# Applying RMS norms behind the products they feed, and moving adaLN modulation chunks to VectorE

## The reference

```
m = silu(cond) @ w_mod[layer] + b_mod[layer]        # 6 x 1024: shift, scale, gate for each of two sub-layers
h = rms_norm(x, g) * (1 + scale) + shift
layer 0: x += gate * even_mixer(h);   x += gate * swiglu(h)             # FF: 1024 -> 2816 -> 1024
layer 1: x += gate * odd_mixer(h);    x += gate * top2_of_8_experts(h)  # a router reads h
y = rms_norm(x, g_f)
rms_norm(x, g) = x * rsqrt(mean(x * x) + eps) * g
```

## Time and profile before

| | |
|---|---|
| time, median of 3 runs | 2267.85 us (2267.14 to 2271.6) |
| time of the profiled execution | 2261.82 us |
| its span | 2260.2 us, mean granted clock of TensorE 0.926 |
| matmuls and transposes | 12138 records on PE |
| DMA | 288 MB, 128 GB/s over the span |

### The profile page before, as it was taken

One profiled execution on the slowest core, in us unless ns is written; L12 is line 12 of the kernel. 1 busy time (PEld: TensorE's weight loads), 2 busy tenths in 40 slices (PEclk: granted clock), 3 DMA queues, 4 the chain that ended last, 5 costly groups with the idle time before them and its releaser, 6 DMA issues.

```text
span 2260.2 us, 34401 instructions
## 1 busy us (share of the span) xinstructions
PE 1978.4 (88%) x12138; PEld 1691.3 (75%) x12139; DVE 1144.8 (51%) x1934; ACT 759.0 (34%) x1265; POOL 327.8 (15%) x344
## 2 busy tenths in 40 slices
PE   4699999999999999987878974997797988887985
PEld 2495586999999986953333943997786988887983
DVE  1436733223322323157886455346575877685435
ACT  1325322222122222222232341334443655553321
POOL 1301102000000002059600020001101001101021
PEclk9799999999999999997687997998998999998996
DMA  7323425335521244223000142357756889866433
GB/s 217 112 75 118 143 80 181 102 85 139 148 75 49 77 139 146 76 95 96 0 1 0 38 123 82 95 159 199 227 146 197 232 240 272 244 182 174 113 91 137
DMA packets 439474, 288.38 MB, mean 128 GB/s; under 512 B 20858, under 2 KB 428634, under 8 KB 439300
## 3 DMA queue, kind: packets, MB, share of 16 engines
q1 hardware_dynamic: 425124, 248.75, 37.9%
q0 software_dynamic: 12272, 34.50, 5.2%
q10 hardware_dynamic: 1904, 3.13, 0.5%
HBM read 262.86 MB, written 23.47 MB: 127 GB/s over the span
## 4 chain that ended last, share of the span: by engine, by line
PE 73%; DVE 13%; issue 8%; ACT 2%; POOL 2%; DMA 1%; ACTq 1%; DVEq 1%; POOLq 0%
PE ps L1076 15%; PE ps L1078 15%; PE ps L1077 15%; PE ps L1081 11%; PE ps L1082 4%; PE ps L1119 4%; DVE vp L1928 2%; PE ps L1169 2%; PE ps L1382 1%; DVE lo L1670 1%; PE ps L1399 1%; POOL tmp L2314 1%; DVE am L1989 1%; DVE hot L2129 1%; PE ps L1493 1%
## 5 line engine op out<-in xcount | busy, mean ns | idle before, releaser
L1076 PE MATMUL ps<-h_both,hi 128*128 128x320 f32 x1728 | 541.8, 314 | 43.2 <-issue 24.2
L1670 DVE TENSOR_TENSOR lo<-raw,hi 128x1024 fp32r<-128x1024 f32 (+3 forms) x442 | 452.4, 1051 | 179.0 <-ACT hi L674 175.3
L1077 PE MATMUL ps<-h_both,hi 128*128 128x320 f32 x1728 | 539.1, 312 | 0.0
L1078 PE MATMUL ps<-h_both,lo 128*128 128x320 f32 x1728 | 538.7, 312 | 0.0
L674 ACT ACTIVATE hi<-raw 128x1024 fp32r<-128x1024 f32 (+3 forms) x442 | 397.1, 919 | 386.7 <-PE ps L1078 233.2
L1076 PEld LDWEIGHTS ps<-h_both,hi 128*128 128x128 f32 x1728 | 328.8, 190 | 47.5 <-issue 34.1
L1081 PE MATMUL ps<-h_both,hi 128*128 128x256 f32 (+2 forms) x1056 | 294.7, 366 | 59.7 <-issue 50.0
L1077 PEld LDWEIGHTS ps<-h_both,hi 128*128 128x128 f32 x1728 | 329.2, 191 | 0.2 <-issue 0.2
L1078 PEld LDWEIGHTS ps<-h_both,lo 128*128 128x128 f32 x1728 | 329.0, 190 | 0.0
L1081 PEld LDWEIGHTS ps<-h_both,hi 128*128 128x128 f32 x1056 | 210.5, 199 | 69.8 <-issue 51.3
L1082 PE MATMUL ps<-h_both,lo 128*128 128x128 f32 (+2 forms) x1056 | 257.1, 243 | 0.0
(11 more groups left out here) (315 smaller groups left out, 2414.9 us busy)
## 6 DMA issues: line engine op xcount, KB each, us to landing
raw<-in_moe_w_dram SPq DMA_DIRECT2D x160, 512.0 KB, 5.4
raw<-in_w_mod_dram SPq DMA_DIRECT2D x96, 512.0 KB, 4.5
raw<-in_moe_w_dram SPq DMA_DIRECT2D x64, 384.0 KB, 3.6
raw<-in_ff_w_dram SPq DMA_DIRECT2D x40, 512.0 KB, 5.0
raw<-in_moe_w_dram SPq DMA_DIRECT2D x64, 320.0 KB, 3.7
y_rows<-zeros POOLq DMA_DIRECT2D x22, 512.0 KB, 4.5
raw<-in_moe_w_dram SPq DMA_DIRECT2D x32, 256.0 KB, 2.9
raw<-in_ev_w_in_dram SPq DMA_DIRECT2D x12, 512.0 KB, 4.5
```

The lines of the kernel that those rows point to most:

```text
L1076: pe.matmul(out, w_hi, v_hi, start=first, stop=False, skip_group_check=True)
L1077: pe.matmul(out, w_hi, v_lo, start=False, stop=False, skip_group_check=True)
L1078: return pe.matmul(out, w_lo, v_hi, start=False, stop=last, skip_group_check=True)
L1670: dve.tensor_tensor(lo[c % 2][:, parts[h]], raw[ring_of(c) % 4][:, parts[h]], hi[c % 2][:, parts[h]].bitcast(F32), ALU.subtract).then_inc( ...
```

## The change

Three things are done together.

1. **Norms 0, 1 and 2 are applied behind the product.** h is x·`amod` without `rs`: ACT writes the high part straight from `xT` (`scaled_hi`, two segments), DVE the low part (`scaled_lo`, two STT, scalar_tensor_tensor). POOL's step and x·rs are gone. The eviction multiplies PSUM by `rs` on DVE (`raw_out`; in FF in `ff13_evac`). `rs` is made while the first step runs; PE waits for `n_var` ahead of half 1, as the sums of norms 1 and 2 now lie in banks 2 and 3. Norm 3 keeps its place, but its affine part moves from POOL to DVE and ACT.
2. **The shift goes through the product as two more moving columns.** `h_wide` has eight columns ahead of the 640; the last two hold the shifts of the two kinds of token, so half 0 has 322 columns, and shift·W comes out beside the product. DVE copies it to `bias`; ACT adds it in place (Identity, Gelu, Sigmoid, or in FF the SiLU), and in FF a DVE STT adds the other one and takes the product.
3. **32 of the 48 chunks leave PE's row form.** Chunks 0 to 7 and 12 to 19 stay. Chunks 8 to 11 are done in EIN's steps 0 to 3, and 20 to 47 in FF's steps `FF_STEPS` (of 38: 1, 3, 5, 7 and 9 to 32), by 16 DVE instructions each (`mod_acc_of`): for both conditioning vectors, over eight k tiles, 256 columns times a scalar per partition, added up. Two steps on, ahead of half 1, PE adds over partitions with four fp32 matmuls (`mod_sum`: 128x128 weights, two columns of ones), and DVE adds b_mod (`mod_bias`). Their weights come through the ring between the product's chunks (`MOD_AT`).

With this PE's loops over FF are written out, squares and ones-matmuls of norm 2 go into FF's last down steps, and the runs of chunks ahead of FF, OIN, the heads and the router are gone. Of the diff, the core:

```diff
+FF_STEPS = [1, 3, 5, 7] + list(range(9, 33))
+BY_PE = list(range(8)) + list(range(12, 20))
+MOD_AT = [0] * 8 + [EIN + 2 + i for i in range(4)] + [EOUT + 2] * 8 + [ff_step(s) for s in FF_STEPS]
+        h_wide = place("h_wide", [P, 2, KT, HW], F32R)
...
+            def scaled_hi(layer, which, k):
+                for lo_t, hi_t, cond in SEGS:
+                    last = act.activation(hh[:, k, lo_t:hi_t], xT[:, k, lo_t:hi_t], ACT.Identity, scale=amod[:, layer, which, k, cond:cond + 1])
+                last.then_inc(n_hi, 1)
...
+            for k in range(4):
+                square(1, k, (evac, 2 * (EOUT + k // 2 + 1)))
+            act.wait_ge(gemm_out, 2 * (EOUT + 4))
+            shift_hi(1, 0, 1)
+            for k in range(KT):
+                if k < 6:
+                    scaled_hi(0, 1, k)
+                if k < 4:
+                    square(1, 4 + k, (evac, 2 * (EOUT + (4 + k) // 2 + 1)))
...
+                    act.wait_ge(f_raw, at + h + 1)
+                    for lo_t, hi_t, cond in HALF_SEGS[h]:
+                        part = sil(h)[:, lo_t - TH * h:hi_t - TH * h]
+                        last = act.activation(part, part, ACT.Silu, bias=bias[:, 0, 0, cond:cond + 1])
...
+            def mod_sum(q, bank):
+                pe.wait_ge(mod_acc, among(q) + 1)
+                for i in range(2):
+                    for c in range(2):
+                        at = 336 + 4 * i + 2 * c
+                        last = pe.matmul(ps[:, bank, at:at + 2], acc_of(q)[:, c, i * P:(i + 1) * P], ones[:, 0:2], start=True, stop=True, skip_group_check=True)
+                last.then_inc(mod_summed, 1)
...
                 for h in range(2):
+                    if h and ready:
+                        pe.wait_ge(n_var, 2)
+                    if h and q < JT and summed_in(s) is not None:
+                        mod_sum(summed_in(s), bank + 2)
...
+                for m in range(KT):
+                    ff2(m, n0 + N_UP + m, s0 + JT + m, 2 * JT * (f + 1), 2 * (n0 + JT - 1) if m < 2 else None)
+                    if f and m >= 2:
+                        norm_mm(2, m - 2)
+
+            norm_mm(2, KT - 2)
+            norm_mm(2, KT - 1)
...
-            mods(28, 2)
-            pe.wait_ge(evac, 2 * OIN)
-            norm_pe(2)
-            mods(30, 2, True)
...
+            def mod_acc_of(q):
+                r = ring_of_mod(q)
+                w = raw[r % 4][:, :].rearrange("p (k c) -> p k c", k=KT)
+                if among(q) >= 2:
+                    dve.wait_ge(mod_summed, among(q) - 1)
+                for k in range(KT):
+                    if k % (KT // 2) == 0:
+                        dve.wait_ge(slot_in[r % 4][k // (KT // 2)], 16 * landed(r))
+                    for c in range(2):
+                        out = acc_of(q)[:, c]
+                        if k == 0:
+                            ins = dve.tensor_scalar(out, w[:, k, :], cs[:, k, c:c + 1], None, ALU.mult)
+                        else:
+                            dve.wait_ge(mod_step, steps[0] - 1)
+                            ins = dve.scalar_tensor_tensor(out=out, in0=w[:, k, :], scalar=cs[:, k, c:c + 1], in1=out, op0=ALU.mult, op1=ALU.add)
...
+            def scaled_lo(i, layer, which, k):
+                dve.wait_ge(n_hi, KT * i + k + 1)
+                for lo_t, hi_t, cond in SEGS:
+                    last = dve.scalar_tensor_tensor(out=hl[:, k, lo_t:hi_t], in0=xT[:, k, lo_t:hi_t], scalar=amod[:, layer, which, k, cond:cond + 1],
+                                                    in1=hh[:, k, lo_t:hi_t].bitcast(F32), op0=ALU.mult, op1=ALU.subtract)
...
+            for c in range(6):
+                raw_out(c, EIN + c, c, z_even)
+                split_lo(EIN + c + 2)
+                if c < 4:
+                    mod_acc_of(8 + c)
+                if c >= 2:
+                    conv_in(c - 2)
...
+                if at:
+                    dve.wait_ge(f_lo, at)
                 for h in range(2):
-                    dve.wait_ge(f_silu, 2 * JT * f + 2 * j + h + 1)
-                    dve.tensor_tensor(gf(h), sil(h), ps[:, 4 * (j % 2) + 2 * h + 1, 0:TH], ALU.mult).then_inc(evac, inc)
+                    dve.wait_ge(gemm_out, 2 * (n + (j == JT - 1)) + h + 1)
+                    off, cols = 2 - 2 * h, slice(h * TH, (h + 1) * TH)
+                    if h == 0:
+                        dve.tensor_copy(bias[:, 0], ps[:, bank:bank + 2, 0:2])
+                    dve.tensor_tensor(sil(h), ps[:, bank + 2 * h, off:off + TH], rs[:, cols], ALU.mult).then_inc(f_raw, 1)
+                    if h and q is not None:
+                        mod_bias(q, bank + 2)
+                    dve.tensor_tensor(gf(h), ps[:, bank + 2 * h + 1, off:off + TH], rs[:, cols], ALU.mult).then_inc(evac, inc)
...
+                        last = dve.scalar_tensor_tensor(out=gf(h)[:, part], in0=gf(h)[:, part], scalar=bias[:, 0, 1, cond:cond + 1],
+                                                        in1=sil(h)[:, part], op0=ALU.add, op1=ALU.mult)
...
+                for j in range(10):
                     ff13_evac(n0 + j, j, f)
-                    split_lo(n0 + j + 2)
+                    split_lo(n0 + j + 2, 0, WHOLE if j < 8 else PART)
+                    if j == 9:
+                        split_lo(n0 + N_UP, 0, DOWN)
+                    accumulate(s0 + j)
...
-            norm_pool(1, 0, 1)
...
-            norm_pool(2, 1, 0)
```

More of the change, by code:

```diff
@@ L709, in _, with square @@
             mod_row(4, 2)
+            def square(i, k, ready):
+                if k >= 4:
+                    act.wait_ge(n_mm, KT * i + k - 3)
+                act.wait_ge(*ready)
+                act.activation(tmp[:, k % 4, 0:T], xT[:, k, :], ACT.Square).then_inc(n_sq, 1)
             def squares(i, ready):
                 for k in range(KT):
[L713 to L723, removed]
+                    square(i, k, ready(k))
+            def root(i):
                 act.wait_ge(n_var, i + 1)
                 act.activation(rs[:, :], rs[:, :], ACT.Sqrt).then_inc(n_std, 1)
-                if first is not None:
-                    first()
-                for k in range(KT):
-                    act.wait_ge(n_aff, KT * i + k + 1)
-                    act.activation(hh[:, k, :], tmp[:, k % 2, 0:T] if h is None else h[:, k, :], ACT.Copy).then_inc(n_hi, 1)
-                    if with_k is not None and k % 2:
-                        with_k(k // 2)
+            def shift_hi(i, layer, which):
+                act.wait_ge(mod_set, i + 1)
+                act.activation(sh_h, mod[:, layer, 24 * which:24 * which + KT, :], ACT.Copy).then_inc(n_shift, 1)
@@ new lines, in mod_bias, with mod_gain @@
+            def mod_bias(q, bank):
+                layer, j0 = q // N_MOD, 2 * (q % N_MOD)
+                v = ps[:, bank, 336:344].rearrange("p (i c d) -> p i c d", i=2, c=2)
+                for c in range(2):
+                    last = dve.tensor_tensor(mod[:, layer, j0:j0 + 2, c], v[:, :, c, 0], par[:, 0, 48 * layer + j0:48 * layer + j0 + 2], ALU.add)
+                link(last)
+            def mod_gain(layer, part):
+                g0 = (N1, N2)[part] + KT * layer
+                for c in range(2):
+                    last = dve.scalar_tensor_tensor(out=amod[:, layer, part, :, c], in0=mod[:, layer, 24 * part + 8:24 * part + 16, c],
+                                                    scalar=1.0, in1=par[:, 0, g0:g0 + KT], op0=ALU.add, op1=ALU.mult)
+                last.then_inc(mod_set, 1)
@@ new lines, in _, with z_even @@
+            norm_rs(0)
+            split_lo(EIN)
+            split_lo(EIN + 1)
+            mod_params(0, part=0)
+            shift_lo(0, 0, 0)
+            for k in range(KT):
+                scaled_lo(0, 0, 0, k)
+            def z_even(m, lo_t, hi_t, cond):
+                s0 = (0, TP)[cond]
+                if 4 <= m < 8:
+                    return ga[:, m - 4, lo_t:hi_t]
+                buf, p0 = (up, (UA_P, UA_S)) if m < 4 else (ub, (UB_P, UB_S))
+                return buf[:, m % 4, p0[cond] + lo_t - s0:p0[cond] + hi_t - s0]
@@ L1867, in _, with summed_in @@
                 residual_pair(c % 2, EOUT + c, c, 0)
[L1868 to L1871 removed]
+                if c < 3:
+                    split_lo(EOUT + c + 2)
+            shift_lo(1, 0, 1)
+            for k in range(KT):
+                scaled_lo(1, 0, 1, k)
+            split_lo(FF + 1)
+            norm_rs(1)
+            def summed_in(s):
+                return 20 + FF_STEPS.index(s - 2) if s - 2 in FF_STEPS else None
```

457 lines of the change are left out of this document (244 added, 213 removed).

## The result

The changed kernel takes **2179.07 us** (median of 4 runs, 2176.25 to 2183.45), the kernel before 2267.49 beside it: ratio 0.9611, interval 0.9586 to 0.9636. The forecast was 2182, faster.

What follows compares the result with a forecast made beforehand. TensorE, busy 88% of the span, was taken to bound the kernel. The terms summed to −86 from the profiled 2261.8 us: 2176 as profiled, 2182 as a median; range 2145 to 2230.

Steps and rivals of the forecast that it cites:

- The gaps: Ahead of FF and behind it, 48.5 and 44.4 us: to shrink to about 9 and 2.6, −39.5 and −41.8.
- Rival 3: Gaps close only in part: alternating squares and scaling, a half-clock start or the handoff leave 20 us, about 2202; 20%.
- handoff: In FF, from up to down: PE waits in its first down step for g_lo; costed at 0, at most 2 × 1.5.
- rival 5: Chunk weights queue behind a slot that a late accumulation holds, and chunks lengthen FF; about 2268; 2%.
- FF: Feed-forward stage, 466.4 us: PE gains norm_mm 6.4, two more columns 0.9, 28 mod_sums 25; +32.3.
- rival 2: mod_sum is dear: switching to fp32 and back drains PE, 2 us each, +35, about 2217; 15%.
- Rivals 1 and 4: VectorE accumulations set the pace: at twice their elements about 2236, 5%; far below the rows' rate, slower than before, 3%.
- the Trainium skill's rule on two SBUF sources: STT with two non-bf16 SBUF sources has half throughput; 14 of 16 accumulations are of that form; about 2236.
- EIN: First matmul about 4 us earlier, some 9 of the 16 lost come back, −13; four mod_sums +3.8.
- to EOUT: Between EIN and EOUT, 75.4 us: four chunks fewer on PE, conv_in later; +1.5, between −4 and +6.
- attention: Behind OIN: prologue from 61 to 42, 3 given back in the heads; −16, between −19 and −5.
- norm 3: Not folded: POOL leaves its rounds, 14 in place of 20, four chunks go, about 5 more; −11.

Runs made afterwards that it cites:

- fold_only: The changed kernel with the 32 moved chunks put back on PE in row form, no accumulation on VectorE; 2232.4 us, ratio 0.9868.
- before_20_chunks: The kernel before with chunks 20 to 47 left out, norms as before; 2184.0 us with experts 879 in place of 913, 43.8 us shorter up to the router's end.
- acc_first: The changed kernel with the accumulation ahead of the first down chunk's split_lo in the last full up step; 2178.4 us, ratio 0.9634, FF 496.9.
- early: The changed kernel with three VectorE moves around EIN, among them first splits, mod_params and scaled_lo ahead of norm 0's reciprocal; 2172.2 us, ratio 0.9598.
- warm_b: The changed kernel with nine unread matmuls in the attention prologue's wait for the reciprocal and one more behind each of five spreads; prologue 46.0 us.

## Why the prediction was right

**The gaps** were right in sum and mechanism: 8.4 and 3.0 for 9 and 2.6, at clock 1.00, no wait for n_lo in FF's first step. fold_only and before_20_chunks show that this needed both parts. Rival 3 (the gaps close in part) is out but for the handoff, and rival 5 with it: in FF PE waits for g_both alone.

**FF**, +32.3 forecast, +35.2 measured. mod_sum: 28 × 0.9 (15.04 − 14.12 in an up step, 10.57 − 9.68 in a down step), 25.4 where I had 25; of it the matmuls are 0.79 in the chain; a row over FF:

```profile
L1178 PE MATMUL ps<-ones,acc_ff 128*128 128x2 f32 x224 | 26.5, 240 | 0.0
```

224 records in 26.5 us, 0.12 each: the fold's price was the right row to take, and rival 2 is out. Two more columns: 0.04 us a step of 96 matmuls, 1.0 in all (0.9). norm_mm 5.4 inside FF (6.4). FF's first step, 14.39 in place of 15.69, −1.3, which I had not counted: before, its granted clock was 0.89, now it is 1.00. And the **handoff, 4.65, which I had at 0 and at most 3**: the step of the sum that failed is "I cost it at 0". I summed DVE's step as a load (12.8 of 15.0) and priced the chain behind the last half, but not that the accumulation stands behind a `split_lo` that waits for the middle of the next step; acc_first showed it. Nor had I the half clock behind the wait, some 1.5 of the 4.65.

**VectorE.** 6.1 a chunk (6.2), 74% busy (70 to 75). Rivals 1 and 4 are out: 0.40 us for an STT of 256, against 0.69 needed for slower. By the Trainium skill's rule on two SBUF sources (Vector Engine (DVE) Microarchitecture Reference, section Points that are easy to get wrong) it would have been about 0.67, an estimate from the page's rule and the 0.267 of the earlier trace rows; the trace disagrees.

**EIN, to EOUT, attention, norm 3**: −10.7, +2.7, −16.9, −12.6 for −9.2, +1.5, −16, −11. Two of these agree only as sums. For EIN I had the first matmul 4 us earlier, "as the reciprocal is no longer ahead of it"; it came 2.0 earlier, for at norm 0 the reciprocal (4.17 us) still stands ahead of `split_lo` and `scaled_lo` in DVE's queue, and once early had moved it, the first matmul came 1.9 earlier. EIN itself made up for that: 8.6 shorter, where I had 5.2. For attention I had the prologue 19 shorter and the heads 3 longer; they are 14.3 and 2.6 shorter. The heads vary: with unchanged code attention as a whole took 246.8 to 255.0 in the later profiles, which would be −18 to −10, so that −16.9 lies so near −16 is luck. And in the prologue the reason was incomplete: half of PE's clock went with the chunks. Giving back part of it (warm_b, 0.83) gained nothing, as DVE's operations beside POOL then took longer.

**The experts**, +7.7 for 0, and the median. The profile of before lies 6 us under its median and I added that; that of after lies 4.4 above. The two offsets of some 10 us and the experts' 7.7 nearly cancel: that 2182 is 3 us from 2179 is partly luck. That the gaps and FF came within 3 us is not luck, as the parts of their sums agree too, but for the handoff.

## What to carry to other kernels

Two slow things that run side by side, a relay between engines and work that fills its waits, each look free; take away both or neither, and work out the gap from what is left. When work goes to an engine's idle time, write out the order of that engine's queue for the steps at a change of phase: a sum of loads that fits says nothing of an instruction that stands behind a wait. Work that was taken off an engine may also have kept its clock up, and added instructions changed waits a thousand us behind them: read the granted clock and the "issue" waits of stages that were not touched.

## What was not expected of the hardware

- The experts' waits for nothing shown, 74 us before and 81 after, moved by 12 us with 14 matmuls more in TensorE's program far ahead of them, in three kernels (42.3, 42.5, 42.9 against 54.4 to 54.6), and the count of `instruction` packets moved with them (84 against 90).
- In attention's prologue PE went from a granted clock of 1.00 to 0.50 once the chunks were gone, though it was busy in all of 950 to 960, and the same four records of a spread took 2.43 us, not 1.27.
- DVE's operations of 512 elements with two inputs in SBUF took 682 to 692 without POOL beside them and up to 1430 on average with it; with one input in PSUM, 682 to 692 in both.
